# Hybrid mLSTM and forgetting-attention trunk on one core: constants of the first head set by GpSimd, events of the first and the last head moved, the preparation reordered

## What is computed

```python
def mlstm_layer(...):
    xm, z = jnp.split(rmsnorm(x, norm_g) @ w_in, 2, axis=-1)
    xc = silu(causal_conv(xm, conv_buf, conv_w, conv_b))
    q = xc_h @ wq;  k = (xc_h @ wk) * 512 ** -0.5;  v = xm_h @ wv
    gates = concat(q, k, v) @ w_gate + b_gate       # ig, lf = log_sigmoid
    # per head: d = exp(log_d - m_t), a = exp(inter - m_t)
    s = (q k^T) * d
    num = s @ v + a * (q @ C);  den = sum(s) + a * (q . n)
    h = num / max(|den|, exp(-m_t))
    C_new = decay * C + sum(w k v^T);  n_new = decay * n + sum(w k)
    h = (head_layernorm(h) * out_g + skip * xc) * silu(z)
    return x + h @ w_out
```

## Time and profile before

| | us |
|---|---|
| median of three runs | 1692.38 |
| the profiled execution, its own time | 1692.91 |
| its span in the trace | 1691.1 |
| TensorE busy | 1661.6 (98%) |
| TensorE weight loads busy | 1593.3 (94%) |
| VectorE busy | 1079.6 (64%) |
| ScalarE busy | 804.6 (48%) |
| GpSimd busy | 298.0 (18%) |

### The profile page before, as it was taken

How to read it: one execution, slowest core, us unless ns; L and a number is a source line. 1 busy time by engine, 2 the same in 40 slices (tenths; PEclk the granted TensorE clock), 3 DMA queues, 4 the chain that set the end, 5 groups by cost and what they waited for, 6 DMA issues and landing times.

```text
span 1691.1 us, 29469 instructions
## 1 busy us (share of the span) xinstructions
PE 1661.6 (98%) x11873; PEld 1593.3 (94%) x11873; DVE 1079.6 (64%) x2080; ACT 804.6 (48%) x1339; POOL 298.0 (18%) x574
## 2 busy tenths in 40 slices
PE   7999999999998999999999999999999999999998
PEld 6999999999997999999999989999999998999998
DVE  5856655655557868768687698566436636563755
ACT  4545344544554534435344445455444554545443
POOL 1102220122132322223222212021112000000000
PEclk9999999999999999999999999999999999999999
DMA  6546554655485766666666545366567654554533
GB/s 184 171 138 217 167 179 142 200 180 179 140 274 170 216 226 180 227 188 210 231 188 224 189 159 183 113 210 203 159 212 261 196 160 153 171 181 156 161 110 109
DMA packets 244232, 309.26 MB, mean 183 GB/s; under 512 B 14008, under 2 KB 219600, under 8 KB 244096
## 3 DMA queue, kind: packets, MB, share of 16 engines
q1 hardware_dynamic: 214352, 215.32, 41.7%
q0 software_dynamic: 29200, 91.23, 15.8%
q10 hardware_dynamic: 544, 0.82, 0.2%
HBM read 260.53 MB, written 46.79 MB: 182 GB/s over the span
## 4 chain that ended last, share of the span: by engine, by line
PE 89%; DVE 5%; ACT 3%; issue 1%; DMA 1%; SPq 0%; ACTq 0%; DVEq 0%
PE acc L177 24%; PE acc L178 24%; PE acc L179 24%; PE aux L1437 3%; PE aux L1288 2%; PE aux L1410 2%; DVE w_lo L157 1%; PE aux L1293 1%; ACT w_hi L152 1%; DMA raw<-in_a_w_in 1%; PE aux L1267 1%; PE aux L2679 1%; PE aux L1444 1%; PE aux L1456 1%; PE aux L2086 1%
## 5 line engine op out<-in xcount | busy, mean ns | idle before, releaser
L157 DVE TENSOR_TENSOR w_lo<-raw,w_hi 128x1024 fp32r<-128x1024 f32 x400 | 485.7, 1221 | 379.3 <-ACT w_hi L152 377.8
L177 PE MATMUL acc<-xg_hi,w_hi 128*128 128x304 f32 x1536 | 473.7, 308 | 2.3 <-issue 1.7
L179 PE MATMUL acc<-xg_hi,w_lo 128*128 128x304 f32 x1536 | 465.1, 303 | 0.0
L152 ACT ACTIVATE w_hi<-raw 128x1024 fp32r<-128x1024 f32 x400 | 414.0, 1055 | 106.7 <-PE acc L179 80.3
L178 PE MATMUL acc<-xg_lo,w_hi 128*128 128x304 f32 x1536 | 464.3, 302 | 0.0
L177 PEld LDWEIGHTS acc<-xg_hi,w_hi 128*128 128x128 f32 x1536 | 290.6, 189 | 4.6 <-issue 1.8
L178 PEld LDWEIGHTS acc<-xg_lo,w_hi 128*128 128x128 f32 x1536 | 291.6, 190 | 0.9
L179 PEld LDWEIGHTS acc<-xg_hi,w_lo 128*128 128x128 f32 x1536 | 291.0, 189 | 0.0
L104 POOL TENSOR_TENSOR cell<-cell 1x1 f32<-1x1 f32 x159 | 73.3, 461 | 1119.7 <-DVE xc_lo L868 322.6
L177 PE MATMUL acc<-xb_hi,w_hi 128*128 128x288 f32 x512 | 156.3, 305 | 0.9 <-DVE w_lo L157 0.9
L177 PE MATMUL acc<-hz_hi,w_hi 128*128 128x304 f32 x512 | 156.1, 305 | 0.4 <-DVE zs L929 0.4
(11 more groups left out here) (499 smaller groups left out, 3005.8 us busy)
## 6 DMA issues: line engine op xcount, KB each, us to landing
raw<-in_a_w_in SPq DMA_DIRECT2D x128, 512.0 KB, 3.9
raw<-in_a_w_out SPq DMA_DIRECT2D x64, 512.0 KB, 4.4
raw<-in_w_kvf SPq DMA_DIRECT2D x64, 512.0 KB, 4.6
raw<-in_b_w_in SPq DMA_DIRECT2D x64, 512.0 KB, 4.6
raw<-in_b_w_out SPq DMA_DIRECT2D x32, 512.0 KB, 3.5
raw<-in_a_wq SPq DMA_DIRECT2D x16, 512.0 KB, 3.8
raw<-in_a_wk SPq DMA_DIRECT2D x16, 512.0 KB, 3.6
raw<-in_a_wv SPq DMA_DIRECT2D x16, 512.0 KB, 4.9
```

The lines of the kernel that those rows point to most:

```text
L152: act.activation(w_hi[:, s, :, :], raw[:, s, :, :], ACT.Copy).then_inc(hi_made, 1)
L157: dve.tensor_tensor(w_lo[:, s, :, :], raw[:, s, :, :], w_hi[:, s, :, :].bitcast(F32), ALU.subtract).then_inc(lo_made, 1)
L177: pe.matmul(acc[b][:, 0:width], wh, x_hi[:, k0 + k, :], start=st, stop=False)
L179: mm = pe.matmul(acc[b][:, 0:width], wl, x_hi[:, k0 + k, :], start=False, stop=last and k == 3)
```

## The change

Five things. (1) Preparation: GpSimd issues the parameter loads after five blocks are turned and the gate weights after all sixteen; SyncE's chunk 1 goes ahead of the second quarter of x; ScalarE loads the ends in three pieces; BESIDE0 is spread over five chunks; for n < 2 the blocks come ahead of the chunk part on ScalarE and VectorE; squares of tile 0 come at n = 2 and of tiles 1 and 2 at n = 3. (2) Seams: the gate products of head 6 come after last_z[:4]; those of head 7 are split, each part waiting only for its own acc buffers (last_taken). (3) Head 0: the pads are set by GpSimd after g_act 6, the zeros of hn after g_cols 2; E, P and Q stand beside the first z chunk, D with set_old_fold beside the second, N with M at the fourth, K at the fifth. (4) norm is split into norm (N) and normed (M), and the last head's E, P, Q, D stand beside head 6's last four z chunks (END_Z), V, K, O one to two chunks earlier, N and M ahead of add_out of chunks 4 and 5, T2 one chunk earlier. (5) Waits: outputs waits for aq_made for the old state's part and for p_lo_made, v_lo_made behind it; exponents waits for den_ready.

```diff
-        TURN0, BESIDE0 = range(0, 4), {0: range(4, 8), 1: range(8, 11), 2: range(11, 14), 3: range(14, 16)}
+        TURN0, BESIDE0 = range(0, 4), {0: range(4, 6), 1: range(6, 9), 2: range(9, 12), 3: range(12, 14), 4: range(14, 16)}
...
-        BESIDE_Z = {0: "N", ...}
-        FIRST_NEXT = {0: "E", 1: "P V Q", 2: "D O K Z", 3: "N", 5: "T0 T1", ...}
+        BESIDE_Z = {0: "N M", ...}
+        FIRST_NEXT = {0: "E P Q", 1: "D", 2: "O Z", 3: "N M", 4: "K", 5: "T0 T1", ...}
-        END_OUT = {0: "E", 1: "P", 2: "Q", 3: "V Z D", 4: "O K", 6: "T0 T1",
-                   7: "T2 T3 S0 S1 H0 H1 S2 S3 H2 H3 S4 S5 S6 n S7"}
-        END_BEFORE = {5: "N"}
+        END_Z = {4: "E", 5: "P", 6: "Q", 7: "D"}
+        END_OUT = {0: "Z", 1: "V", 2: "K", 3: "O", 6: "T0 T1 T2", 7: "T3 S0 S1 H0 H1 S2 S3 H2 H3 S4 S5 S6 n S7"}
+        END_BEFORE = {4: "N", 5: "M"}
...
-            FIRST = ("x0", 0, "x1", 1, 2, "x2", 3, "x3")
+            FIRST = ("x0", 0, 1, "x1", 2, "x2", 3, "x3")
...
             for n in range(8):
+                if n < 2:
+                    high_x(BESIDE0[n])
                 high_part(act, Count(n + 2))
-                high_x(BESIDE0.get(n, ()))
-                if n in (1, 2, 3):
-                    squares(n - 1)
+                if n > 1:
+                    high_x(BESIDE0.get(n, ()))
+                for t in {2: (0,), 3: (1, 2)}.get(n, ()):
+                    squares(t)
...
-                    gate_products(Count(LAST - 1))
                 post(Count(LAST - 1), (2 * j, 2 * j + 1))
                 x_products(n, j, tile)
+            gate_products(Count(LAST - 1))
...
                 if j == 4:
-                    tokens_taken(Count(LAST))
-                    gate_products(Count(LAST))
-                    post(Count(LAST), (0, 1, 2, 3))
+                    last_taken(last_qkv[0:4])
+                    gate_products(Count(LAST), (0, 1))
+                    post(Count(LAST), (0, 1))
+                    last_taken(last_qkv[4:6])
+                    gate_products(Count(LAST), (2,))
+                    post(Count(LAST), (2, 3))
...
-                wait(pe, p_lo_made, h + 1)
-                wait(pe, v_lo_made, h + 1)
+                wait(pe, aq_made, h + 1)
                 wait(pe, C_landed, (h + 1).times(16))
...
+                wait(pe, p_lo_made, h + 1)
+                wait(pe, v_lo_made, h + 1)
...
+            pool.wait_ge(turned, 5)
             for _, src, t, r0, n in PARAMS:
...
-            gates_in(Count(0))
             pool.wait_ge(taken, KD)
+            gates_in(Count(0))
...
             pool.wait_ge(g_act, 6)
+            pool.memset(cols[:, :, :], 1.0).then_inc(pads_set, 1)
+            pool.memset(aq[:, :], 0.0).then_inc(pads_set, 1)
+            pool.memset(P_hi[:, :].bitcast(F32), 0.0).then_inc(pads_set, 1)
+            pool.memset(P_lo[:, :].bitcast(F32), 0.0).then_inc(pads_set, 1)
...
             pool.wait_ge(g_cols, 2)
+            pool.memset(hn[32:64, 2, :], 0.0).then_inc(pads_set, 1)
+            pool.memset(hn[64:P, 2, :], 0.0).then_inc(pads_set, 1)
```

More of the change, by code:

```diff
@@ L341, in trunk @@
              "v_hi_made", "vt_hi_made", "v_lo_made", "k_hi_made", "kt_hi_made", "k_lo_made",
-             "den_ready", "den_taken", "den_in", "old_ready", "old_hi_made", "old_lo_made", "n_ready", "n_taken", "var_ready", "root_made",
+             "den_ready", "den_taken", "den_in", "aq_made", "old_ready", "old_hi_made", "old_lo_made", "n_ready", "n_taken", "var_ready", "root_made",
              "gated", "hz_hi_made", "hz_ready", "head_set", "pads_set"))
@@ L581, in squares @@
                 if t == 0:
-                    for b, count in enumerate((80, 80, 32, 32)):
+                    for b, count in enumerate((80, 80, 80, 32)):
                         act.wait_ge(x_in[b], count)
@@ L904, in mix_vector @@
             for n in range(8):
+                if n < 2:
+                    parts_of(BESIDE0[n])
                 low_part(dve, Count(n + 2))
-                if n in BESIDE0:
+                if n > 1 and n in BESIDE0:
                     parts_of(BESIDE0[n])
@@ L1043, in exponents @@
                 wait(dve, p_lo_made, h)
-                wait(dve, b_ready, h.times(USES))
+                wait(dve, den_ready, h)
                 wait(dve, S_landed, h.times(S_LOADS) + (S_LOADS - 16))
@@ L1079, in sums @@
                 wait(dve, p_lo_made, h + 1)
+                wait(dve, aq_made, h + 1)
                 own.wait()
@@ L1092, in sums, with set_old_fold @@
                 dve.tensor_tensor(tail, tail, aq_sum[:, :], ALU.add).then_inc(den_in, 1)
-            def low_old(h):
[L1095 to L1100, removed]
+            def set_old_fold():
+                own.done(dve.memset(fold[:, :].bitcast(F32), 0.0))
+                own.wait()
+                for r in range(0, P, DEC):
+                    own.done(dve.tensor_copy(fold[r:r + DEC, 16:TAIL], ident[r:r + DEC, r:r + DEC]))
+                own.wait()
+            def low_old(h):
                 wait(dve, old_hi_made, h + 1)
@@ L1121, in norm @@
             def norm(h):
-                if (h.a, h.b) == (0, 0):
-                    own.done(dve.memset(hn[32:64, 2, :], 0.0))
-                    own.done(dve.memset(hn[64:P, 2, :], 0.0))
+                wait(dve, pads_set, 6)
                 wait(dve, den_ready, h + 1)
@@ L1203, in event @@
                     sums(h)
+                    if (h.a, h.b) == (0, 0):
+                        set_old_fold()
                 elif e == "V" and (h.a or h.b):
@@ L1212, in event @@
                     norm(h)
+                elif e == "M":
+                    normed(h)
                 elif e[0] == "T":
@@ L1258, in tokens_taken, with last_taken, gate_products @@
                     wait(pe, acc_free[b], h.times(4) + (5 if not last or b < 2 else 4))
-            def gate_products(h):
+            def last_taken(steps):
+                for _, _, tile in steps:
+                    for u in (tile, tile + 1):
+                        wait(pe, acc_free[u.turn(4)], u.rounds(4) + 1)
+            def gate_products(h, sources=(0, 1, 2)):
                 wait(pe, wg_landed, (h + 1).times(48))
-                for g, src in enumerate((q_T, k_T, v_T)):
+                for g in sources:
                     for d in range(HT):
                         r = 32 * d
-                        mm = pe.matmul(gate_sum[r:r + 32, 0:T], wg_in[:, HT * g + d, :], src[:, d, :],
+                        mm = pe.matmul(gate_sum[r:r + 32, 0:T], wg_in[:, HT * g + d, :], (q_T, k_T, v_T)[g][:, d, :],
                                        start=h.a == 0 and g == 0, stop=h.a == LAST and g == 2, skip_group_check=True,
                                        tile_position=(0, r))
-                mm.then_inc(gates_made, 1)
+                if 2 in sources:
+                    mm.then_inc(gates_made, 1)
             def fold_gates():
```

40 lines of the change are left out of this document (22 added, 18 removed).

## The result

The changed kernel takes 1682.2 us (median of 4 runs, 1681.52 to 1682.68). The kernel before, timed beside it, takes 1693.36 (1692.04 to 1695.48). The ratio is 0.993, 95% interval 0.9918 to 0.9941. That is 11.2 us off where 10.4 were forecast, and the time is 0.2 us from the number predicted. The parts of the sum did not all come out, though, as the traces show. The profiled execution of the changed kernel took 1681.52 us, its span is 1679.7 against 1691.1.

A forecast was written before the change was run, and what follows sets the result against it. TensorE is busy 98%, so only its stops and lowered clock can be won. 2.0 + 1.0 + 1.0 + 2.3 + 4.2 = 10.5 off 1692.9 gives 1682.4, against the median 1682.0; range 1678.0 to 1688.0.

The forecast's parts named there:

- The clock holds: Rival, head 0: the clock does not fall and old_lo is less late, 1.7 to 3 us more off, 1679.5; chance 0.20.
- The stops only move: Rival: the next late thing takes most of heads 0 and 7, 2 us left of each, 1687.5; chance 0.16.
- The 18 us: Ceiling of the change: 11.6 us of TensorE's waits plus 6.8 us of lowered clock behind three long stops.
- 1.: Preparation: the xT stop and its clock loss go, new stops come at the seventh chunk and behind; 2.0 us off.
- The walk: Stepping through the three queues with the trace's durations; in the preparation it put new stops at 1.7, 0.8 and 0.8 us.
- 2.: Head 6's gate products, moved later, fill the stop for xc_lo: 1.0 us off, bounds 0 and 1.2.
- 3.: Head 7's split gates cover the 1.0 us wait for v_T and nothing queued there becomes late: 1.0 us off.
- 4.: Head 0's outputs: E, P and Q run together, 4.0 us earlier less 1.7 for the clock: 2.3 us off.
- the charge of 1.7 for one stretch at 1.2 GHz: Head 0: 1.7 us charged for a clock fall behind two stops forecast at 0.7 and 1.9 us.
- held behind one low part: Head 0: if GpSimd's memsets are held behind one VectorE low part, the pads end near 504.9 and the sum stays.
- 5.: Last head: steps moved up cut stops and clock loss from 4.9 us to 0.7: 4.2 us off, ends 2 and 4.9.
- 6.: Middle heads and waits: no TensorE stop stands at the changed waits, so 0 us.

The follow-up runs named there:

- e9: The kernel before, unchanged, in a second trace: 1689.95 us in one execution; nine runs beside it gave 1694.39 us.
- e8: The changed kernel with the squares of the three tiles one each behind chunks 1, 2 and 3: 1684.25 us, ratio 0.9946.
- e2: The changed kernel with head 0's steps in the old order (E; P V Q; D O K Z; N M): 1684.16 us, ratio 0.9942.
- e5: The changed kernel with the four pads on VectorE and E alone in the first chunk, P, V and Q in the second: 1683.93 us, ratio 0.994.
- e10: The changed kernel, unchanged, timed and traced again (its trace is "changed again"): 1683.45 us, ratio 0.9934.
- e3: The changed kernel with VectorE taking head 7's score pairs ahead of the chunk's low part and the gate sums' copy: 1680.34 us, ratio 0.992.
- e1: The changed kernel with only the four pads set by VectorE again, behind the last z tiles: 1683.41 us, ratio 0.9934.
- e6: The changed kernel with the last head's steps as before, its pairs and norm not moved up: 1686.51 us, ratio 0.9957.
- e7: The changed kernel with ScalarE's second load of the ends issued only behind the samples' landing: 1687.32 us, ratio 0.9957.
- e11: The changed kernel with the edits of e3 and e8 together: 1681.18 us, ratio 0.9921.
- e12: As e5, with TensorE's waits for P's and V's low halves again ahead of the old-state products, every head: 1686.13 us, ratio 0.9951.
- e4: The changed kernel with the fold matrix set ahead of the exponents, not behind the sums: 1680.45 us, ratio 0.9919.

## Why the prediction was right, and where it was not

**The number held because errors of both signs met, which is luck.** Forecast per part against the traces: preparation 2.0 and 1.4 (with its start); head 6's gates 1.0 and 0.9; head 7's 1.0 and none; head 0 2.3 and 4.45; last head 4.2 and 3.4; nothing and 1.55 for the keys and values. The rival *The clock holds* is what the traces show in head 0; its 1679.5 did not come, since head 7's gates, the last head and the preparation gave 2.4 less than their forecasts. The 1687.5 of *The stops only move* does not follow from its terms: with 2 us left of head 0 and the last head, 7 to 8 us come off and not the 4.9 that 1687.5 stands for.

**What bounds it, and the ceiling.** The reading that only TensorE's stops and its clock can be won held. The 18 us counted the clock at its face value, 6.8 us. e9 shows what three of four falls, the one at 1080 among them, are worth: 3.1 us. A fall costs little where another engine sets the pace behind it, as in the last head.

**1.** The stop for xT and the clock fall went. Of the 2.0 us between chunks 0 and 8, 1.16 are the fall, by e9. The walk found each stop in its place, and made them twice as long as they are. It called the one for w_lo new, where the kernel before already stopped 0.68 us, so only 0.84 us of stops were added (0.12, 0.44 and 0.28). The reason, the squares of two tiles together, is what e8 bears out: apart, the two stops of 0.80 and 0.44 shrink to 0.26 at that place. But 0.72 comes up earlier, so having them together costs 0.35 us. The late start of chunk 0, 0.45, is no cost of the change for certain: e2, e5 and e10 start it at 10.84 to 11.03.

**2.** Right to 0.1: 1.70 off ahead, 0.80 of it paid back where the products now lie. No run takes this edit, or the preparation's as a whole, back alone; here the stretches of the traces speak.

**3.** Wrong. The step that failed is "nothing queued there becomes late". The walk looked at who needs the last gates (fold_gates), not at what stands behind their copy (L986) in VectorE's queue: the copy of S_st, which frees the bank for TensorE's transposes. e3 takes the pairs ahead of both and gets the 1.04 us. The wait that was to be covered was also read as 1.0 us: that is the longest of the two for v_T, which is the one at 433 that stays; the one here was 0.87.

**4.** The walk without the clock gave 4.0, the traces 4.45; the two stops, 0.24 and 1.61, lie within half a microsecond of the 0.7 and 1.9 forecast. The step that failed is the charge of 1.7 for one stretch at 1.2 GHz. It did not come in either trace of the changed kernel, yet it came, at 1.53 to 1.56 us, in e1, e6 and e7 behind nearly the same stops (0.3 to 0.5, then 1.6) and in e8 behind 1.76 and 1.6, and did not come in e11 behind 1.08 and 1.6. So the reason given (1.9 us lies nearer to the 2.5 that lost the clock than to the 1 that didn't) does not hold: the clock held behind 2.57 us in e2 and 3.10 in e5. The charge was a chance and should have been taken as one. As to causes within the 4.45: the start of E 0.27, the order of the steps 1.35, the waits placed singly with the clock 1.7, the settings nothing or 0.1 by E's start, and 1.0 to 1.1 left, which by e9 against e12 goes to hn's zeros on VectorE. The prediction named the microsecond of VectorE that they take, but gave its removal no term in the sum. That a_row and not the pads starts E is so in the changed kernel (a wait of 1.66 us); with the pads on VectorE the two are a near tie (E waits 0.14 us for a_row in the kernel before, and follows VectorE's own copies in e1 and e9). The bound "held behind one low part" was not met either: the four memsets took 0.65, 0.35, 0.66 and 0.58 us beside a low part that kept its 1.2, and ended at 502.1, ahead of both forecasts. This agrees with the section "SBUF: two separate sides" of the Trainium skill's SBUF — State Buffer. VectorE's column copies did wait for the pads, 0.32 us here and 1.25 in e8, inside the wait for a_row. The price taken from the row of 304 columns was too high: 2.0 us for 2128 columns, from 500.1, and not 2.6.

**5.** The mechanism held, the term of the clock was mis-sized: 1.7 counted, 0.42 found by e9. Then 2.9 would have been forecast; the traces give 3.4 and, without clock falls on either side (e9 to changed again), 3.2. The stops that were forecast, 0.2 and 0.5, are 0.27 and 0.15, and the one of 0.58 for skip_in was not forecast. In e9 the kernel before stops 0.22 and 0.45 for skip_in itself: with the clock up, VectorE sets the pace there, which is why the fall cost 0.42 and not 1.7. By stops alone e9 has 3.8 us there and the changed kernel again 0.74, 3.1 of the 3.2. In e6 the old steps cost 4.5 us in the trace, with 6.8 us at half clock, and 3.2 to 3.5 in the run at full clock.

**6.** No stop moved at the singly placed waits of the middle heads (419.96 us from chunk 130 to 226 in both). The 1.55 us at the keys and values were not in the prediction. No edit lies there, and e9 shows the kernel before without them.

**How much is the change's own.** Both second traces are free of the falls in the preparation, the last head and the keys and values; e9 keeps one in head 0. They differ by 1688.1 - 1678.8 = 9.3 us. The 24 timed runs of the kernel before beside the experiments all had a mean clock of 0.994 to 0.996, the nine of the changed kernel 0.998 to 1.000. So, by an estimate from these two traces, 8 to 9 us of the 11 are stops taken away, and the rest is clock that the changed kernel keeps more often. Why it keeps it is not settled: no run here sets the stops apart from the clock.

## What to carry to other kernels

When a piece of work is moved later on one engine, follow every queue in which something waits for it and read what stands behind that waiter; the reader that needs the result last is not the one that sets the cost. Price a clock fall by what would bound the stretch without it, and as a chance: take a second trace of the same kernel before charging or crediting it. Where a stage starts with a load whose landing varies, measure from that start on, or the landing is taken for the edit (e4, e5). Small edits are best judged by a stretch between two fixed instructions, where 0.05 us can be read, and not by medians that the start and the clock shift by 1 to 3 us.

## What the runs showed of the hardware

**The same stop, with and without a clock fall.** At the keys and values TensorE stops for 0.6 to 0.7 us in every trace, in front of the same instructions. Kernel before, then the changed kernel again:

```profile
1077.90 1.54 PE L2128 MATMUL aux<-ident,rstd_row 128*128 128x1 f32 x12 [0.63 <-DVE ntmp L2005]
```

```profile
1066.98 1.54 PE L2159 MATMUL aux<-ident,rstd_row 128*128 128x1 f32 x12 [0.69 <-DVE ntmp L2036]
```

Behind it the next chunk's stretch (249 to 250) took 10.59 to 10.65 us in seven traces (before, e1, e2, e5, e7, e8, e12), with the clock at 0.5 for over 3 us, and 9.09 or 9.10 in the other seven (changed, e3, e4, e6, e9, e10, e11), with the clock at 1.00. So a stop of 0.7 us came with 1.55 us more in half of the traces, and stops of 2.57 (e2) and 3.10 us (e5) in head 0 with nothing more.

**Landing times vary.** From a_row's issue to E, the first operation that reads it, took 3.9 us in the changed kernel's trace, 4.6 in e11, 4.9 in e4 and 5.3 in e8. Chunk 0 began between 10.84 us (e5) and 13.20 us (e12) in traces whose code up to there is the same.

**Issuing a load can hold the engine that does it for over a microsecond.** In e7 one issue on ScalarE took 1.62 us, where the first ones take 0.43. What made it long is not shown.
